# Moving the operands of a decoder layer's products by 16, 64 and 128 bytes in SBUF

## The chip, the cores and the metric

The kernel runs on one core of a Trainium2 chip. The metric is the device time of one execution in microseconds; a run's figure is the median over several executions. TensorE is PE in the profile (PEld its weight loads), VectorE is DVE, ScalarE is ACT, GpSimd is POOL, SyncE is SP.

## The reference

One decoder layer on 512 tokens of width 1024, all in float32: a shared RMS norm, one combined input projection, eight heads of block-sparse attention and four of differential attention, an output projection with a residual, and a SwiGLU feed-forward with 2816 hidden columns. The change touches where the feed-forward's operands lie, so its lines matter most:

```python
h = rms_norm(x, attn_norm[l])
proj = jnp.einsum('bsd,de->bse', h, w_in[l])
...
mixed = jnp.concatenate([moba_out, diff_out], axis=-1)
x = x + jnp.einsum('bse,ed->bsd', mixed, w_out[l])
h = rms_norm(x, ffn_norm[l])
g = jnp.einsum('bsd,df->bsf', h, w_gate[l])
u = jnp.einsum('bsd,df->bsf', h, w_up[l])
x = x + jnp.einsum('bsf,fd->bsd', jax.nn.silu(g) * u, w_down[l])
```

## The kernel before

Every float32 product is made of three matmuls on parts: an operand is split into a high part (a rounded copy, written by ACT) and a low part (the rest, written by DVE), and `product` issues high by high (line 1575), high by low (1576) and low by high (1577). Each of the three loads a 128 by 128 block of weights into the array (the stationary operand) and streams the other operand past it (the moving one). So each matmul reads two places of SBUF at about the same time: its moving operand, and the weights of the matmul behind it.

The weight parts lie in two rings of four slots, `w_hi` (WH) and `w_lo` (WL), 1024 float32 to a slot and partition. Product n uses slot n modulo 4 of both. ACT writes a slot of WH as soon as PE is done with its last user, DVE then the same slot of WL. The engines run written-out programs and wait on semaphores; no scheduler orders them.

Three stages follow each other on PE:

1. Projections and attention. Weights are slots 0 to 2 of the rings, the moving operand is `h_parts` (H1), 512 columns at a time. Short attention matmuls lie between. The output projection then takes `mixed_parts` (MIX) as weights, and ring slots, `w_out_parts` or H1 as the moving operand.
2. Gate and up, 78 products of 24 matmuls (1872 in all) by a seven-product scheme in `gate_product` and `first_product`. Weights are ring slots; the moving operand is 256 tokens of `h_first_parts` (A1: products Q1 and Q2) or one of five sums in `h_sum_parts` (SC: index 0 for Q6, 1 for Q5, 2 for Q7, 3 for Q3, 4 for Q4). Ten of the eleven units run all seven products; in each of them three, Q5, Q7 and Q3, use the sums 1, 2 and 3. The first unit's eight products run plainly, four of them on A1, two on sum 3 and two on sum 4. Beside PE, DVE and ACT split the weights of the products to come and add blocks of weights (`w_sum`).
3. Down, 42 steps in `down`. Here the hidden activations' parts, `hidden_parts` (AR), are the weights and the ring slots are the moving operand, 512 columns at a time.

Tensors are placed by hand, one behind the other, with byte offsets in a partition. `place` hands out the next offset or takes one that is given; `r0` is the offset of H1:

```python
WH, at_wh = place("w_hi", [P, 4, D], F32R)
WL, at_wl = place("w_lo", [P, 4, D], F32R)
...
SHIFT = 320
SC, _ = place("h2_sum_parts", [P, 5, 2, KTH, HALF], F32R, r0 + SHIFT)
A1, _ = place("h2_first_parts", [P, 2, KT, HALF], F32R, r0 + 106 * KB + SHIFT)
AR, _ = place("hidden_parts", [P, SLOTS, 2, SEQ], F32R, r0 + 106 * KB + 512)
```

A block of weights is 512 bytes of a partition, a moving operand 1024 bytes (256 columns) or 2048 bytes (512 columns), and the blocks and operands within a slot or a sum follow each other at these distances. Worked out from the first offset, 16512, each operand begins at these remainders of 512 bytes: WH and WL 128 in all four slots, H1, MIX, `w_out_parts` and AR 128, SC 448 in all five sums, A1 448.

Of the kernel before, what the change touches and what calls it, by code (L numbers as in the profile page):

```python
# [36 lines left out]
F32 = mybir.dt.float32  # L37
F32R = mybir.dt.float32r
U32 = mybir.dt.uint32

P = 128
SEQ = 512
D = 1024
# [5 lines left out]
KT = D // P  # L49
PAIRS = 8  # L50
MOBA_PAIRS = 4
FT = FFN // P
# [33 lines left out]
HALF = SEQ // 2  # L86
KTH = KT // 2
SLOTS = 4

assert FT % 2 == 0  # L90
assert SEQ // BLOCK == 2, "MoBA is causal attention for two blocks only"

# [54 lines left out]
def build(nc, x, wt, vec, gain2, lams, ident_in, mask_in, cos_in, sin_in, out):  # L147
    with ExitStack() as ctx:
        cursor = [16512]

        def place(name, shape, dt, at=None):

            n = 4
            for s in shape[1:]:
                n *= s
            if at is None:
                at = cursor[0]
                cursor[0] += n
            return nc.alloc_sbuf_tensor_at(name, shape, dt, offset=at), at

        def sem(name):
            return ctx.enter_context(nc.semaphore(name))


        X, _ = place("residual", [P, TT, D], F32)
        RAW, _ = place("w_raw", [P, 4, D], F32)
        WH, at_wh = place("w_hi", [P, 4, D], F32R)
        WL, at_wl = place("w_lo", [P, 4, D], F32R)
        ident, _ = place("ident", [P, P], F32)
        mask, _ = place("mask", [P, P], F32)  # L170
        cosT, at_cos = place("cos", [P, SEQ], F32)
        sinT, _ = place("sin", [P, SEQ], F32)
        small, _ = place("small", [P, 256], F32)

        QG, at_tmp = place("q_gained", [P, SEQ], F32)
        QR, _ = place("q_rotated", [P, SEQ], F32)
        QS, _ = place("q_roped", [P, SEQ], F32)
        KG, _ = place("k_gained", [P, SEQ], F32)
        KR, _ = place("k_rotated", [P, SEQ], F32)
        KS, _ = place("k_roped", [P, SEQ], F32)  # L180
        VT, _ = place("v_by_dim", [P, SEQ], F32)
        C1, _ = place("q1_kept", [P, SEQ], F32, at_tmp)
        V3, _ = place("q167_kept", [P, SEQ], F32, at_tmp + 2048)
        V2A, _ = place("q16_kept_0", [P, SEQ], F32, at_tmp + 2 * 2048)
        G0, _ = place("gate_first", [P, SEQ], F32, at_tmp + 3 * 2048)
        T1, _ = place("w_sum_1", [P, D], F32, at_tmp + 4 * 2048)
        U1, _ = place("up_second", [P, SEQ], F32, at_tmp + 6 * 2048)
        WO, _ = place("w_out_parts", [P, 2, D], F32R, at_tmp)


        KB = 1024
        SHIFT = 320
        H1, r0 = place("h_parts", [P, KT, 2, SEQ], F32R)
        MIX, r1 = place("mixed_parts", [P, KT, 2, SEQ], F32R)
        SC, _ = place("h2_sum_parts", [P, 5, 2, KTH, HALF], F32R, r0 + SHIFT)
        LATE = [place(f"down_raw_{n}", [P, D], F32, r0 + (4 * n if n < 5 else 34) * KB)[0] for n in range(6)]
        SN, _ = place("hidden_sums", [P, UNITS, HALF], F32, r0 + 22 * KB)
        RAW1, _ = place("w_raw_odd", [P, 4, D], F32, r0 + 40 * KB + SHIFT)
        G1, _ = place("gate_second", [P, SEQ], F32, r0 + 56 * KB + SHIFT)
        U0, _ = place("up_first", [P, SEQ], F32, r0 + 58 * KB + SHIFT)  # L200
        V2B, _ = place("q16_kept_1", [P, SEQ], F32, r0 + 60 * KB + SHIFT)
        HID, _ = place("hidden", [P, FT, SEQ], F32, r0 + 62 * KB + SHIFT)
        A1, _ = place("h2_first_parts", [P, 2, KT, HALF], F32R, r0 + 106 * KB + SHIFT)
        AR, _ = place("hidden_parts", [P, SLOTS, 2, SEQ], F32R, r0 + 106 * KB + 512)
        T2, _ = place("w_sum_2", [P, D], F32, at_cos)
        V2 = (V2A, V2B)
        r2 = r1 + 32 * KB
        VF, _ = place("v_turned", [P, TT, P], F32, r2)
        QF, _ = place("q_ready", [P, SEQ], F32, r2 + 8 * KB)
        KF, _ = place("k_ready", [P, SEQ], F32, r2 + 10 * KB)  # L210
        SQQ, _ = place("q_squared", [P, SEQ], F32, r2 + 16 * KB)
        SQK, _ = place("k_squared", [P, SEQ], F32, r2 + 18 * KB)
        MSR, _ = place("mean_square_rows", [P, 2, HALF], F32, r2 + 2 * KB)
        KBC, _ = place("k_rstd_spread", [P, TT, 2, HEAD], F32, r2 + 20 * KB)
        ON, _ = place("o_normed", [P, TT, P], F32, r2 + 22 * KB)
        LAM0, _ = place("lambda_in", [P, 4 * HEAD], F32, r2 + 22 * KB)

        HN2, _ = place("h2_normed", [P, TT, D], F32, r2)
        JUNK2, _ = place("squares2", [P, D], F32, r2 + 16 * KB)
        G2, _ = place("ffn_gain", [P, D], F32, r2 + 20 * KB)  # L220

        r3 = r2 + 24 * KB
        H2R, _ = place("h2_by_dim", [P, KT, SEQ], F32, r3)
        SR, _ = place("h2_sums", [P, 4, KTH, HALF], F32, r2 + 2 * KB + SHIFT)
        PT, _ = place("probsT", [P, 2, TT, SEQ], F32, r3)
        JUNK, _ = place("squares", [P, 2, D], F32, r3 + 16 * KB)

        PR0, _ = place("probs_0", [P, 2, SEQ], F32, at_wh + 3 * 4 * D)
        PR1, _ = place("probs_1", [P, 2, SEQ], F32, at_wl + 3 * 4 * D)
        PR = (PR0, PR1)  # L230


# [53 lines left out]
        w_hi = sem("w_hi_ready")  # L286
        w_lo = sem("w_lo_ready")
# [1831 lines left out]
```

## Time and profile before

| what | value |
|---|---|
| median of 3 runs | 602.42 us (602.38 to 602.43) |
| span of the profiled execution | 600.4 us |
| PE busy (matmuls) | 592.0 us, 99% of the span |
| PEld busy (weight loads) | 507.4 us, 85% |
| DVE busy | 471.8 us, 79% |
| ACT busy | 315.3 us, 53% |
| POOL busy | 28.1 us, 5% |
| instructions | 10407, of them 3820 matmuls |

The profile is of one execution. Its time is given by its span alone, from the first instruction to the end of the last; the 2.0 us between 600.4 and the runs' median lie around the program and are in no row. A matmul's row gives its start and a modelled end, and neighbours overlap, so busy time says little about pace. The pace is read from the starts: the distance between two matmuls' starts, divided by the matmuls between them.

### The profile page before, as it was taken

The page shows a single profiled execution, that of the slowest core. Times are in us where ns is not written, and L with a number is a line of the kernel's source. Part 1 is how long each engine was busy: PE and PEld are TensorE (multiplying, and loading weights), DVE is VectorE, ACT ScalarE, POOL GpSimd, SP SyncE. Part 2 cuts the span into 40 slices and gives each one's busy share as a digit, 9 for nine tenths or more (in the row PEclk, how much of TensorE's full clock was granted, in tenths as well). Part 3 has the DMA queues.
Part 4 walks back from the last instruction along what each step waited for, and adds up shares of the span by engine and source line. Part 5 has one row for each costly group of instructions (what it writes and reads, how often), then busy time and mean ns, then how long its engine had stood idle before and what let it go on. Part 6 is the DMA issues. An engine that isn't in the chain of part 4 may idle for free.

```text
span 600.4 us, 10407 instructions
## 1 busy us (share of the span) xinstructions
PE 592.0 (99%) x3820; PEld 507.4 (85%) x3820; DVE 471.8 (79%) x769; ACT 315.3 (53%) x545; POOL 28.1 (5%) x28
## 2 busy tenths in 40 slices
PE   8999999999999999999999999999999999999997
PEld 7766776776777777889999999999999998888886
DVE  4877777776797977677977788778877877999774
ACT  6555647375464646346554445453544365556551
POOL 0000000000000000000000000000000022155200
PEclk9999999999999999999999999999999999999999
DMA  8414132240412243308132243223422479699911
GB/s 298 124 58 136 41 102 70 70 136 6 139 52 89 70 175 106 106 2 281 36 118 80 86 141 134 77 73 141 139 71 73 142 180 264 182 190 206 187 36 70
DMA packets 33240, 70.31 MB, mean 117 GB/s; under 512 B 3376, under 2 KB 3760, under 8 KB 33200
## 3 DMA queue, kind: packets, MB, share of 16 engines
q1 hardware_dynamic: 26896, 58.14, 28.6%
q0 software_dynamic: 6016, 11.54, 10.9%
q8 instruction: 27, 0.44, 0.3%
q14 instruction: 13, 0.11, 0.1%
q10 hardware_dynamic: 288, 0.08, 0.1%
HBM read 63.45 MB, written 2.10 MB: 109 GB/s over the span
## 4 chain that ended last, share of the span: by engine, by line
PE 88%; DVE 6%; ACT 2%; issue 2%; SPq 1%; DMA 1%; DVEq 0%; ACTq 0%
PE ps L1575 26%; PE ps L1576 25%; PE ps L1577 25%; PE ps L1662 2%; PE ps L1680 2%; PE ps L1697 2%; PE ps L1705 1%; DVE small L1100 1%; ACT probs L664 1%; SPq L469 1%; PE ps L1741 1%; DVE probs L1128 1%; DVE ps L1094 1%; PE ps L1932 1%; PE ps L1751 1%
## 5 line engine op out<-in xcount | busy, mean ns | idle before, releaser
L1575 PE MATMUL ps<-h_sum_parts,w_hi 128*128 128x256 f32 x432 | 120.6, 279 | 0.7 <-ACT q_kept L866 0.7
L1576 PE MATMUL ps<-h_sum_parts,w_hi 128*128 128x256 f32 x432 | 120.9, 280 | 0.0
L1577 PE MATMUL ps<-h_sum_parts,w_lo 128*128 128x256 f32 x432 | 120.5, 279 | 0.0
L1575 PEld LDWEIGHTS ps<-h_sum_parts,w_hi 128*128 128x128 f32 x432 | 81.2, 188 | 0.9 <-ACT q_kept L866 0.9
L1576 PEld LDWEIGHTS ps<-h_sum_parts,w_hi 128*128 128x128 f32 x432 | 81.1, 188 | 0.0
L1577 PEld LDWEIGHTS ps<-h_sum_parts,w_lo 128*128 128x128 f32 x432 | 80.8, 187 | 0.0
L1575 PE MATMUL ps<-h_parts,w_hi 128*128 128x512 f32 x190 | 77.9, 410 | 0.3 <-DVE h_parts L1171 0.3
L1577 PE MATMUL ps<-h_parts,w_lo 128*128 128x512 f32 x190 | 74.5, 392 | 0.0
L1576 PE MATMUL ps<-h_parts,w_hi 128*128 128x512 f32 x190 | 74.1, 390 | 0.0
L664 ACT ACTIVATE probs<-ps,small 128x128 f32<-128x128 f32 (+3 forms) x64 | 38.9, 614 | 45.9 <-DVE small L1105 45.8
L1576 PE MATMUL ps<-w_lo,hidden_parts 128*128 128x512 f32 x154 | 59.9, 389 | 0.0
L1575 PE MATMUL ps<-w_hi,hidden_parts 128*128 128x512 f32 x154 | 59.9, 389 | 0.0
L1577 PE MATMUL ps<-w_hi,hidden_parts 128*128 128x512 f32 x154 | 59.9, 389 | 0.0
L1576 PE MATMUL ps<-h_first_parts,w_hi 128*128 128x256 f32 x192 | 53.8, 280 | 0.0
L1575 PE MATMUL ps<-h_first_parts,w_hi 128*128 128x256 f32 x192 | 53.7, 280 | 0.0
L1577 PE MATMUL ps<-h_first_parts,w_lo 128*128 128x256 f32 x192 | 53.6, 279 | 0.0
L1024 DVE TENSOR_TENSOR w_lo<-w_raw,w_hi 128x1024 fp32r<-128x1024 f32 x29 | 35.3, 1222 | 16.4 <-ACT w_hi L616 16.4
L1575 PEld LDWEIGHTS ps<-h_parts,w_hi 128*128 128x128 f32 x190 | 35.7, 188 | 10.2 <-issue 4.0
L1577 PEld LDWEIGHTS ps<-h_parts,w_lo 128*128 128x128 f32 x190 | 35.7, 188 | 8.0
L1576 PEld LDWEIGHTS ps<-h_parts,w_hi 128*128 128x128 f32 x190 | 35.8, 189 | 6.3
L1024 DVE TENSOR_TENSOR w_lo<-w_raw_odd,w_hi 128x1024 fp32r<-128x1024 f32 x25 | 30.6, 1223 | 13.2 <-ACT w_hi L616 13.2
L561 POOL DMA_DIRECT2D w_raw_odd<-wt x12 | 14.6, 1214 | 522.3 <-DVE w_lo L1415 522.3
(189 smaller groups left out, 1232.9 us busy)
## 6 DMA issues: line engine op xcount, KB each, us to landing
w_raw<-wt SPq DMA_DIRECT2D x59, 512.0 KB, 4.5
w_raw_odd<-wt SPq DMA_DIRECT2D x24, 512.0 KB, 4.2
w_raw_odd<-wt POOLq DMA_DIRECT2D x12, 512.0 KB, 7.4
down_raw<-wt SPq DMA_DIRECT2D x6, 512.0 KB, 9.5
w_raw<-wt POOLq DMA_DIRECT2D x5, 512.0 KB, 10.2
residual<-x SPq DMA_DIRECT2D x4, 512.0 KB, 5.1
q_rotated<-q_gained SPq DMA_DIRECT2D x32, 64.0 KB, 2.0
k_rotated<-k_gained SPq DMA_DIRECT2D x32, 64.0 KB, 2.0
```

Source lines behind the costliest of these rows:

```text
L469: sp.dma_start(dst[32 * b:32 * b + 32], src[32 * (b ^ 1):32 * (b ^ 1) + 32]).then_inc(done, 16)
L561: pool.dma_start(down_raw("B11", c).rearrange("p (f n) -> p f n", n=SEQ), down_rows(role, c), accum_op=ALU.add).then_inc(tb_added[c], 16)
L664: nc.scalar.activation(PR[qt % 2][:, a, 0:W], ps[:, 2 + a, at:at + W], ACT.Exp, bias=NB[:, i:i + 1], scale=RQ[:, i:i + 1], accum_out=SUM[: ...
L1024: nc.vector.tensor_tensor(WL[:, n % SLOTS], product_source(n), WH[:, n % SLOTS].bitcast(F32), ALU.subtract).then_inc(c_lo, 1)
L1094: nc.vector.tensor_tensor(diagonal, diagonal, mask[:].unsqueeze(1).unsqueeze(1).broadcast_to([P, 2, blocks, P]), ALU.add).then_inc(masked, 1)
L1100: ins = nc.vector.tensor_reduce(MX[:, 2 * qt:2 * qt + 2], ps[:, 2:4, s0:s0 + (qt + 1) * P], AX.X, ALU.max)
L1575: nc.tensor.matmul(dst, lh, rh, start=start, stop=False, skip_group_check=True)
L1576: nc.tensor.matmul(dst, lh, rl, start=False, stop=False, skip_group_check=True)
L1577: return nc.tensor.matmul(dst, ll, rh, start=False, stop=stop, skip_group_check=True)
L1662: ins = nc.tensor.matmul(ps[:, 2 + a, at:at + W], QF[rows[a], qt * P:W], KF[rows[a], 0:W], start=True, stop=True, skip_group_check=True)
L1680: ins = nc.tensor.transpose(ps[:, bank, at + kt * P:at + (kt + 1) * P], PR[qt % 2][:, a, kt * P:(kt + 1) * P], ident[:])
L1697: ins = nc.tensor.matmul(ps[rows, 6, qs], VF[:, kt, rows], PT[:, a, kt, qs], start=kt == 0, stop=kt == TT - 1, skip_group_check=True)
```

## The change

No instruction is added, removed or moved: on every engine the program's rows are the same, in the same order, and only line numbers differ by up to eight. What changes is addresses. The slots of both rings lie 4160 bytes apart and no longer 4096. The five sums of SC lie 8208 bytes apart and no longer 8192. What lies above SC in the same region (`w_raw_odd`, `gate_second`, `up_first`, `q16_kept_1`, `hidden` and A1) is 128 bytes higher, in which the 80 bytes that SC grows by find room. A gap of 256 bytes behind each ring makes all that follows move by 1024 bytes together.

In remainders of 512 bytes: slots 0 to 3 of WH and of WL now begin at 128, 192, 256, 320; the sums 0 to 4 of SC at 448, 464, 480, 496, 0; A1 at 64. H1, MIX, `w_out_parts` and AR stay at 128. The distance of the moving operand from the weights, in the same remainders, was 320 in stage 2 and 0 in stages 1 and 3. It is now 320 less 64 for each slot and more by 16 for each sum (448 less 64 for each slot with A1) in stage 2, and a multiple of 64 from 0 to 192, by the slot, in those parts of stages 1 and 3 that use the rings. Sums 1, 2 and 3 are the only ones that no longer begin at a multiple of 64 bytes.

```diff
+STEP = 16
+APART = 4
...
-        WH, at_wh = place("w_hi", [P, 4, D], F32R)
-        WL, at_wl = place("w_lo", [P, 4, D], F32R)
+        WH_, at_wh = place("w_hi", [P, 4, D + STEP], F32R)
+        cursor[0] += 4 * 4 * STEP
+        WL_, at_wl = place("w_lo", [P, 4, D + STEP], F32R)
+        cursor[0] += 4 * 4 * STEP
+        WH, WL = WH_[:, :, 0:D], WL_[:, :, 0:D]
...
-        SC, _ = place("h2_sum_parts", [P, 5, 2, KTH, HALF], F32R, r0 + SHIFT)
+        SC_, _ = place("h2_sum_parts", [P, 5, 2 * KTH * HALF + APART], F32R, r0 + SHIFT)
+        SC = SC_[:, :, 0:2 * KTH * HALF].rearrange("p i (a k q) -> p i a k q", a=2, k=KTH)
...
-        RAW1, _ = place("w_raw_odd", [P, 4, D], F32, r0 + 40 * KB + SHIFT)
+        RAW1, _ = place("w_raw_odd", [P, 4, D], F32, r0 + 40 * KB + SHIFT + 128)
...
-        A1, _ = place("h2_first_parts", [P, 2, KT, HALF], F32R, r0 + 106 * KB + SHIFT)
+        A1, _ = place("h2_first_parts", [P, 2, KT, HALF], F32R, r0 + 106 * KB + SHIFT + 128)
...
-        PR0, _ = place("probs_0", [P, 2, SEQ], F32, at_wh + 3 * 4 * D)
-        PR1, _ = place("probs_1", [P, 2, SEQ], F32, at_wl + 3 * 4 * D)
+        PR0, _ = place("probs_0", [P, 2, SEQ], F32, at_wh + 3 * 4 * (D + STEP))
+        PR1, _ = place("probs_1", [P, 2, SEQ], F32, at_wl + 3 * 4 * (D + STEP))
```

## Rows read from the trace of the kernel before

**Rows 1.** The page, parts 1 and 2: busy time, and the granted clock in slices.

```profile
PE 592.0 (99%) x3820; PEld 507.4 (85%) x3820; DVE 471.8 (79%) x769; ACT 315.3 (53%) x545; POOL 28.1 (5%) x28
...
PEclk9999999999999999999999999999999999999999
```

**Rows 2.** Windows by stage: us; busy PE, PEld, DVE, ACT, POOL; granted clock; DMA.

```profile
0.00:20.00 20.00, 18.18 (x92) 15.96 (x93) 11.32 (x23) 12.56 (x21) 0.20 (x4) 1.00 0.69 250
20.00:269.00 249.00, 246.31 (x1378) 182.64 (x1378) 192.18 (x461) 133.11 (x308) 0.00 (x0) 1.00 0.28 87
269.00:486.00 217.00, 217.00 (x1842) 216.75 (x1841) 176.08 (x183) 108.96 (x133) 0.00 (x0) 1.00 0.32 112
486.00:492.50 6.50, 5.81 (x50) 5.74 (x50) 5.12 (x8) 4.16 (x7) 2.54 (x2) 1.00 1.02 256
492.50:601.00 108.50, 104.68 (x462) 86.34 (x460) 87.08 (x99) 56.49 (x78) 25.35 (x22) 1.00 0.74 164
```

**Rows 3.** Timeline of PE in stage 2, start and us; 189 starts apart.

```profile
300.02 0.28 PE L1575 MATMUL ps<-h_sum_parts,w_hi 128*128 128x256 f32 x1
...
322.28 0.28 PE L1575 MATMUL ps<-h_sum_parts,w_hi 128*128 128x256 f32 x1
```

**Rows 4.** Tile h_sum_parts from 310 to 470: duration in ns, min/median/max.

```profile
L1575 PE MATMUL ps<-h_sum_parts,w_hi x324: 279/279/279, 310.6 to 470.0; 128*128 128x256 f32 x162
L1576 PE MATMUL ps<-h_sum_parts,w_hi x323: 280/280/280, 310.7 to 469.7; 128*128 128x256 f32 x162
L1577 PE MATMUL ps<-h_sum_parts,w_lo x323: 279/279/279, 310.9 to 469.9; 128*128 128x256 f32 x162
```

**Rows 5.** Timeline of PE, end of stage 2; the last two are 42 starts apart.

```profile
485.64 0.28 PE L1576 MATMUL ps<-h_sum_parts,w_hi 128*128 128x256 f32 x1
485.76 0.28 PE L1577 MATMUL ps<-h_sum_parts,w_lo 128*128 128x256 f32 x1
486.72 0.39 PE L1575 MATMUL ps<-h_sum_parts,w_hi 128*128 128x256 f32 x1 [0.69 <-ACT q_kept L866]
486.94 0.28 PE L1576 MATMUL ps<-h_sum_parts,w_hi 128*128 128x256 f32 x1
487.06 0.28 PE L1577 MATMUL ps<-h_sum_parts,w_lo 128*128 128x256 f32 x1
487.17 0.28 PE L1575 MATMUL ps<-h_sum_parts,w_hi 128*128 128x256 f32 x1
...
491.93 0.28 PE L1575 MATMUL ps<-h_sum_parts,w_hi 128*128 128x256 f32 x1
```

**Rows 6.** Tile h_sum_parts from 487.5 to 492: duration in ns.

```profile
L1576 PE MATMUL ps<-h_sum_parts,w_hi x14: 276/276/276, 487.3 to 491.7; 128*128 128x256 f32 x14
L1577 PE MATMUL ps<-h_sum_parts,w_lo x14: 276/276/276, 487.4 to 491.8; 128*128 128x256 f32 x14
```

**Rows 7.** Timeline of PE, first matmuls of stage 3; the last row is the twelfth.

```profile
492.27 0.39 PE L1575 MATMUL ps<-w_hi,hidden_parts 128*128 128x512 f32 x1
492.50 0.40 PE L1576 MATMUL ps<-w_lo,hidden_parts 128*128 128x512 f32 x1
492.74 0.39 PE L1577 MATMUL ps<-w_hi,hidden_parts 128*128 128x512 f32 x1
492.97 0.40 PE L1575 MATMUL ps<-w_hi,hidden_parts 128*128 128x512 f32 x1
493.20 0.39 PE L1576 MATMUL ps<-w_lo,hidden_parts 128*128 128x512 f32 x1
...
494.79 0.39 PE L1577 MATMUL ps<-w_hi,hidden_parts 128*128 128x512 f32 x1
```

**Rows 8.** Timeline of PE near the end, 444 starts behind the last row above.

```profile
595.43 0.39 PE L1577 MATMUL ps<-w_hi,hidden_parts 128*128 128x512 f32 x1
```

More of the change, by code:

```diff
@@ L194, in build @@
         MIX, r1 = place("mixed_parts", [P, KT, 2, SEQ], F32R)
-        SC, _ = place("h2_sum_parts", [P, 5, 2, KTH, HALF], F32R, r0 + SHIFT)
+        SC_, _ = place("h2_sum_parts", [P, 5, 2 * KTH * HALF + APART], F32R, r0 + SHIFT)
+        SC = SC_[:, :, 0:2 * KTH * HALF].rearrange("p i (a k q) -> p i a k q", a=2, k=KTH)
         LATE = [place(f"down_raw_{n}", [P, D], F32, r0 + (4 * n if n < 5 else 34) * KB)[0] for n in range(6)]
         SN, _ = place("hidden_sums", [P, UNITS, HALF], F32, r0 + 22 * KB)
-        RAW1, _ = place("w_raw_odd", [P, 4, D], F32, r0 + 40 * KB + SHIFT)
[L199 to L202, printed above, removed]
-        A1, _ = place("h2_first_parts", [P, 2, KT, HALF], F32R, r0 + 106 * KB + SHIFT)
+        RAW1, _ = place("w_raw_odd", [P, 4, D], F32, r0 + 40 * KB + SHIFT + 128)
+        G1, _ = place("gate_second", [P, SEQ], F32, r0 + 56 * KB + SHIFT + 128)
+        U0, _ = place("up_first", [P, SEQ], F32, r0 + 58 * KB + SHIFT + 128)
+        V2B, _ = place("q16_kept_1", [P, SEQ], F32, r0 + 60 * KB + SHIFT + 128)
+        HID, _ = place("hidden", [P, FT, SEQ], F32, r0 + 62 * KB + SHIFT + 128)
+        A1, _ = place("h2_first_parts", [P, 2, KT, HALF], F32R, r0 + 106 * KB + SHIFT + 128)
         AR, _ = place("hidden_parts", [P, SLOTS, 2, SEQ], F32R, r0 + 106 * KB + 512)
```

## The prediction

> **What bounds the kernel now.** First the page: PE is busy for 592.0 of 600.4 us, and its granted clock stands at 9 tenths or more in every slice [rows 1]. So PE bounds the kernel, at its upper level of 2.4 GHz, and the question is whether it is at its best pace.
>
> Then the windows by stage [rows 2]. In stage 2 (269 to 486 us) PE has work for all of 217.0 us, its weight loads for 216.75, DVE for 176 and ACT for 109. DVE has 19% to spare, so no other engine sets the pace there. In stage 3 (492.5 on) PE is again without gaps until the end, and its loads are busy for 86 of 108.5 us. The clock is 1.00 in each window.
>
> Then the starts of matmuls. In stage 2, 189 starts take 322.28 - 300.02 = 22.26 us: 117.78 ns for a matmul of 256 columns [rows 3]. It is the same everywhere: from 310 to 470 us the three kinds of matmul have durations of 279, 280 and 279 ns from minimum to maximum, whatever slot, sum or block they read and whatever DVE and ACT do beside them [rows 4].
>
> But one piece of stage 2 runs faster. Before product Q4 of the last unit PE waits: its last start before is 485.76, the next 486.72, released by ACT's copy of Q7's result. From 487.17 to 491.93 then, 42 starts take 4.76 us: 113.33 ns each [rows 5], and the duration is 276 ns [rows 6]. These are the same instructions, on the same rings and sums at the same remainders of addresses, with the same clock. So **there are two paces for the same matmul**, 4.45 ns apart, and each keeps itself up: the slow one through more than 1800 matmuls, the fast one, after a restart, until the stage ends.
>
> Stage 3 shows what a disturbance costs where the moving operand has 512 columns. From 494.79 to 595.43, 444 starts take 100.64 us, 226.67 ns each, which is twice 113.33 [rows 7, 8]. Its first matmuls come at distances of 0.23, 0.24, 0.23 and 0.23 us, and the first eleven take 494.79 - 492.27 = 2.52 us, where eleven at the even pace take 2.493. So PE needs a few matmuls to settle after the switch from stage 2, and pays some 27 ns for it [rows 7].
>
> **The change, part by part.** Nothing is executed more or less, and no wait moves, so all of it is in the pace at which a pair of reads, weights and moving operand, gets through. The trace of before cannot show what another distance between the two does: all of stage 2 has one distance (320, in remainders of 512), all of stages 1 and 3 another (0). Each cost is therefore bounded from both paces.
>
> Stage 2 at the fast pace. Of 1872 matmuls the last 48 run fast already. The other 1824 give back at most 1824 x 4.45 ns = 8.1 us. The lower bound is 0, and on the side of a loss a second step of the same size, 4.45 ns a matmul. I take the whole 8.1 us as the first term: the slow pace lived on unbroken sameness, and a restart was enough to end it. With the change the distance moves at all 77 switches from one product to the next, since the slot moves on by 64 bytes each time and the sum by 16, 32 or 48 bytes at most switches. That is a disturbance per 24 matmuls, and of the two paces the one that two products of other slot and sum shared without a break [rows 5] is the one that I expect to be found and kept.
>
> What the switches cost. A settling of 27 ns [rows 7] at each of 77 switches is 2.1 us. Bounds: 0 (the switch between the last two products, within rows 5, leaves 113.33 untouched) and twice as much, 4.2 us. I take 2.1, since now the distance changes too.
>
> Stage 3. The ring slots are the moving operand, and the distance changes at each of 41 switches between 42 steps. The even pace of 226.67 may stay for all distances; a settling of 27 ns at each switch costs 1.1 us. Bounds: 0 and 2.2 us. I take 1.1.
>
> Stage 1. The projections' three blocks of a pair change slot too, but attention matmuls break them up already and PE settles anew after each break, so I take 0, with up to 24 x 27 ns = 0.6 us against it.
>
> The other moves cost nothing: `w_raw_odd`, `hidden`, `gate_second`, `up_first`, `q16_kept_1` and the two tiles of probabilities are read by DVE, ACT, PE's transposes and DMA as before. If DVE's or ACT's instructions grew by a few per cent, the 41 us that DVE has free in stage 2 [rows 2] would hide it. A faster PE asks DVE for 176 us of work in some 211 instead of 217, which leaves 35. The wait before the last unit's Q4, 0.96 us from start to start, follows from PE's own result and ACT's copy of it [rows 5], and stays.
>
> The sum: -8.1 + 2.1 + 1.1 = -4.9 us. Against the profiled execution, 600.4 - 4.9 = 595.5 us of span; with the 2.0 us by which the median of the runs lies above that span, 597.5 us.
>
> A page speaks against all this. What the rows show: one matmul, two paces, with no other engine's work to tell them apart [rows 4, 5]. The Trainium skill, "SBUF — State Buffer", section "Who interferes with whom", says that PE has two read ports, one for the moving operand and one for weights, independent of each other, and that PE never waits on anyone there. By it no address matters, the sum would be 0 and the time 602.4. The trace does not contradict it outright, since no row has the same stage at two distances; but two ports without any interplay leave the second pace unexplained.
>
> **The rivals.**
>
> *No change.* The paces depend on how PE entered the stage, not on where the operands lie; 117.78 ns stays. For it: both paces occur at the same addresses [rows 3, 5], and the small stop within the first product, for transposes, did not bring the fast one, since rows 3 come after it. Against it: at a fixed distance nothing could shake the pace off. It gives 602.4 us, within 0.2%, which is about what a measurement of this kernel can tell from no change.
>
> *Slower: the sums off the 64-byte grid.* The sums 1, 2 and 3 begin 16, 32 and 48 bytes behind a multiple of 64, which no operand of PE does before. If a moving row that straddles such a multiple costs one more step of 4.45 ns, the 32 products on these sums pay 768 x 4.45 = 3.4 us, and if no fast pace comes to pay for it, the time is 605.8. It decides from 1.6 ns a matmul on (1.2 us, the 0.2%). For it: the kernel's only even paces were measured with everything on that grid. Against: the rows know just two paces and no third.
>
> *All of it.* The fast pace comes and the switches cost nothing, as between the last two products: 602.4 - 8.1 = 594.3 us.
>
> *A part.* Only some products leave the slow pace, say those of one or two slots of four, a quarter to a half of 8.1 us, less the switches: about 600.
>
> **How the numbers follow.** The forecast (fast pace with settling) has a chance of 0.40, its own range 594.3 to 600.5, the latter if settling costs twice the terms above (8.1 - 6.4 = 1.7). All of it 0.10, a part 0.08, no change 0.17, slower 0.25. Faster by over 0.2% takes the first three, 0.58; same is 0.17; slower 0.25. The range runs from 593.8, a little under the full gain, to 605.8, the slower rival's own time; it leaves out some 0.15, most of it losses larger than one step, as in stage 3, where 462 matmuls at 4.45 ns more would add 2.1 us.
>
> **What would show each step.** The first term: in the profile after, starts of stage 2 at 113.3 ns and durations of 276 ns for most products. Settling: one to five uneven distances behind each switch of product or step, and an even pace between. The slower rival: Q5, Q7 and Q3 alone at more than 117.8 ns. No change: 279 and 280 ns as before. The prediction is wrong if the fast pace needs the old distance: then every product has a pace of its own by slot and sum, and the time is a mean over them that no row of before holds.

## The result and the profile after

The changed kernel takes 606.05 us (605.27 to 606.23, 4 runs) against 602.4 us (601.7 to 602.43, 4 runs) for the kernel before: 1.0062 times, 95% interval 1.005 to 1.0074. It is slower by 0.6%; 597.5 us were predicted. The profiled execution is the fastest of the four (605.27), so the traces show 3.1 us of the 3.65 between the medians.

The page, parts 1 and 2, as in [rows 1]:

```profile
PE 595.7 (99%) x3820; PEld 507.0 (84%) x3820; DVE 472.2 (78%) x769; ACT 315.5 (52%) x545; POOL 28.1 (5%) x28
...
PEclk9999999999999999999999999999999999999999
```

PE is busy for 3.7 us more, DVE and ACT for 0.4 and 0.2, and the clock stands as before. So PE's own matmuls grew. Where they did is read from windows that end at the first matmul of each stage (columns as in [rows 2]). First the changed kernel, then the kernel before:

```profile
10.55:269.79 259.24, 257.33 (x1416) 190.31 (x1417) 201.76 (x479) 140.56 (x321) 0.00 (x0) 1.00 0.28 91
269.79:493.33 223.54, 222.85 (x1890) 222.65 (x1888) 180.82 (x189) 113.19 (x139) 2.54 (x2) 1.00 0.34 116
493.33:603.50 110.17, 106.96 (x464) 86.55 (x462) 87.45 (x99) 56.54 (x78) 25.32 (x22) 1.00 0.73 161
```

```profile
10.67:269.29 258.62, 255.67 (x1416) 189.94 (x1417) 201.59 (x479) 140.47 (x321) 0.00 (x0) 1.00 0.29 91
269.29:492.27 222.98, 222.29 (x1889) 222.09 (x1888) 180.69 (x189) 113.08 (x139) 2.54 (x2) 1.00 0.34 116
492.27:600.40 108.13, 104.91 (x464) 86.53 (x462) 87.31 (x99) 56.52 (x78) 25.35 (x22) 1.00 0.75 165
```

Stage 1 is 0.62 us longer, stage 2 0.56, stage 3 2.04. Together, with a start 0.12 earlier, that is the 3.1 us between the spans of 600.4 and 603.5. PE's waits did not grow: in each stage the busy time rose by as much as the length, or by more.

The tile `h_sum_parts` from 310 to 470 us, which answers to [rows 4], and `hidden_parts` from 495 to 595; duration in ns, minimum/median/maximum:

```profile
L1583 PE MATMUL ps<-h_sum_parts,w_hi x322: 275/281/288, 311.1 to 470.0; 128*128 128x256 f32 x161
```

```profile
L1583 PE MATMUL ps<-w_hi,hidden_parts x145: 388/394/398, 494.7 to 594.6; 128*128 128x512 f32 x145
```

Where one duration stood before, a whole band stands now, 13 ns wide in stage 2. What lies in it is seen in the timeline of PE (start and us). The first six rows are three pairs, each 15 starts apart within one product on `h_first_parts`: product 20 on ring slot 0, product 27 on slot 3, product 34 on slot 2. The last six are the first matmuls of steps of stage 3, 12 starts apart, on slots 2, 3, 0, 1, 2 and 3:

```profile
328.86 0.28 PE L1583 MATMUL ps<-h_first_parts,w_hi 128*128 128x256 f32 x1
...
330.56 0.28 PE L1583 MATMUL ps<-h_first_parts,w_hi 128*128 128x256 f32 x1
...
348.64 0.28 PE L1583 MATMUL ps<-h_first_parts,w_hi 128*128 128x256 f32 x1
...
350.44 0.28 PE L1583 MATMUL ps<-h_first_parts,w_hi 128*128 128x256 f32 x1
...
368.51 0.28 PE L1583 MATMUL ps<-h_first_parts,w_hi 128*128 128x256 f32 x1
...
370.21 0.28 PE L1583 MATMUL ps<-h_first_parts,w_hi 128*128 128x256 f32 x1
...
493.33 0.39 PE L1583 MATMUL ps<-w_hi,hidden_parts 128*128 128x512 f32 x1
...
496.11 0.39 PE L1583 MATMUL ps<-w_hi,hidden_parts 128*128 128x512 f32 x1
...
498.91 0.39 PE L1583 MATMUL ps<-w_hi,hidden_parts 128*128 128x512 f32 x1
...
501.65 0.40 PE L1583 MATMUL ps<-w_hi,hidden_parts 128*128 128x512 f32 x1
...
504.41 0.40 PE L1583 MATMUL ps<-w_hi,hidden_parts 128*128 128x512 f32 x1
...
507.21 0.39 PE L1583 MATMUL ps<-w_hi,hidden_parts 128*128 128x512 f32 x1
```

15 starts take 1.70 us (113.3 ns each) in product 20, 1.80 us (120.0) in product 27, and 1.70 again in product 34. The three products read the same half, so one moving operand has different paces on different ring slots. In stage 3 the steps take 2.80 us on slot 3 (233.3 ns), 2.74 on slot 0 (228.3), 2.76 on slot 1 (230.0) and 2.80 on slot 2, where the even pace of before was 226.67 [rows 8].

**The theories.** The distance theory (D): the pace of a matmul follows from the distance between its moving operand and the weights, taken in remainders of some power of two, and lasts as long as that distance does. Its rivals: only the switches cost (each change of slot or sum brings a settling, and the pace between is as before); a moving operand off the 64-byte grid costs a step; and, for the two paces of before, a stop of PE ends the slow one. Distance below is the moving operand's first byte less the weights' first byte, as a remainder of 512 unless another is named.

### The profile page after: what moved, and what is told of

It is laid out like the page before. It is cut to its first block, busy times and chain, and to the rows that moved or that the text cites. A ratio compares the mean times of both kernels' runs of the same rounds, so it can differ in the third digit from the quotient of the medians.

```text
span 603.5 us, 10407 instructions
## 1 busy us (share of the span) xinstructions
PE 595.7 (99%) x3820; PEld 507.0 (84%) x3820; DVE 472.2 (78%) x769; ACT 315.5 (52%) x545; POOL 28.1 (5%) x28
## 4 chain that ended last, share of the span: by engine, by line
PE 88%; DVE 6%; ACT 2%; issue 1%; DMA 1%; SPq 1%; DVEq 0%; ACTq 0%
PE ps L1583 26%; PE ps L1585 26%; PE ps L1584 26%; PE ps L1670 3%; PE ps L1688 2%; PE ps L1705 2%; PE ps L1713 1%; DVE small L1108 1%; ACT probs L672 1%; DMA residual<-x 1%; DVE probs L1136 1%; DVE ps L1102 1%; PE ps L1627 1%; PE ps L1940 1%; PE ps L1654 1%
```

## The experiments

### e1: the rings alone

The slots of the rings 64 bytes further apart, the sums and `h2`'s first half where they were. Against the changed kernel:

```diff
-APART = 4
+APART = 0
...
-        A1, _ = place("h2_first_parts", ..., r0 + 106 * KB + SHIFT + 128)
+        A1, _ = place("h2_first_parts", ..., r0 + 106 * KB + SHIFT)
```

> The rings' slots stand 64 bytes further apart, the sums and the first half stay where they were. Theory D (a matmul's pace is set by the distance from its weights to its moving operand, in remainders of 512 bytes): stages 1 and 3 lose what they lose with the whole change (0.6 and 2.1 us); in stage 2 the products run at 117.8, 120.0, 117.7 or 113.4, and 118.8 ns for slots 0 to 3, which adds 1.5 us or takes 0.5: 604.6 to 606.6 in all. Theory S (my prediction's: every switch of distance costs a settling of some 27 ns, and an even distance costs nothing): 77 and 41 switches, 605 to 606. Theory G (only operands off the 64-byte grid are slow): nothing is off the grid, so stage 2 keeps 117.8 and the time is 602.4 if stage 3 keeps its pace too.

604.85 us (604.62 to 605.31) against 601.94: 1.0047 (1.003 to 1.0063). The timeline of PE at the first matmuls of five products in a row, 24 starts apart, on slots 0, 1, 2, 3 and 0:

```profile
328.49 0.28 PE L1583 MATMUL ps<-h_first_parts,w_hi 128*128 128x256 f32 x1
...
331.32 0.28 PE L1583 MATMUL ps<-h_sum_parts,w_hi 128*128 128x256 f32 x1
...
334.20 0.28 PE L1583 MATMUL ps<-h_first_parts,w_hi 128*128 128x256 f32 x1
...
336.93 0.28 PE L1583 MATMUL ps<-h_sum_parts,w_hi 128*128 128x256 f32 x1
...
339.77 0.28 PE L1583 MATMUL ps<-h_sum_parts,w_hi 128*128 128x256 f32 x1
```

The products take 2.83, 2.88, 2.73 and 2.84 us. Their distances are 320, 256, 192 and 128, and every product of a slot has its slot's pace, whatever sum it reads: 117.8, 120.0, 113.3 and 118.7 ns in the even part (the intervals repeat in a short pattern, on slot 1 for example 121, 120, 124, 118, 117 ns, and the pace is the mean over whole patterns). The four nearly cancel: stage 2 is 222.82 us long, 222.98 before. Stage 3, where the distance goes 0, 64, 128, 192, is 110.17 us, just as after the whole change. So the rings alone hold the loss of stage 3, and all operands here lie on the 64-byte grid. The time by itself fits the theory of switches as well (605 to 606); what decides against it is that the paces differ in the even parts, between the switches.

### e2: the sums alone

The complement: the sums 16 bytes further apart and `h2`'s first half 128 further on. Against the changed kernel:

```diff
-STEP = 16
+STEP = 0
```

> The sums stand 16 bytes further apart and the first half 128 bytes further on, the rings are as before. D: stages 1 and 3 are as before, since their distances are; in stage 2 sum 0 runs at 117.8, sum 1 at 119.7, sum 2 at 119.9, sum 3 at 113.3, sum 4 at 119.0 and the first half at 117.8 or 113.4 ns, a mean of 117.9 or 116.7: 602.7 or 600.4. S: some 50 switches in stage 2, 1.4 us, 603.8. G: sums 1 to 3 alone are slower, each by the same step, others keep 117.8.

601.58 us (600.61 to 602.1): 0.9994 (0.9984 to 1.0003). PE's timeline at the first matmuls of Q3 (sum 3), Q6 (sum 0), Q5 (sum 1), Q7 (sum 2) and the product behind them:

```profile
335.08 0.28 PE L1583 MATMUL ps<-h_sum_parts,w_hi 128*128 128x256 f32 x1
...
337.84 0.28 PE L1583 MATMUL ps<-h_sum_parts,w_hi 128*128 128x256 f32 x1
...
340.67 0.28 PE L1583 MATMUL ps<-h_sum_parts,w_hi 128*128 128x256 f32 x1
...
343.55 0.28 PE L1583 MATMUL ps<-h_sum_parts,w_hi 128*128 128x256 f32 x1
...
346.43 0.28 PE L1583 MATMUL ps<-h_first_parts,w_hi 128*128 128x256 f32 x1
```

2.76, 2.83, 2.88 and 2.88 us at distances 368, 320, 336 and 352. Now the pace goes with the sum and not with the slot. Of the three sums off the grid, two are slower than before and one, sum 3, is the fastest (113.3 ns in its even part, with some 35 ns a product for settling). The off-grid rival asked for all three to be slower, and so falls. The time lies between the two that D had named, since `h2`'s first half, at 448, runs at 113.3 ns in 12 of its products and at 117.8 in the others. Stage 3 is 108.10 us, as before.

### e3: one distance, 368, for all of stage 2

If the distance decides, then all products at the distance of sum 3 are fast, with no slot moved. The kernel before with the sums and `h2`'s first half at a remainder of 496 (their neighbours are moved out of the way by `SHIFT`; `SC` and `A1` are views that begin 4 floats into their tensors):

```diff
-        SHIFT = 320
+        SHIFT = 512
...
-        SC, _ = place("h2_sum_parts", [P, 5, 2, KTH, HALF], F32R, r0 + SHIFT)
+        SC_, _ = place("h2_sum_parts", [P, 5 * 2 * KTH * HALF + 4], F32R, r0 + 352)
+        SC = SC_[:, 4:4 + 5 * 2 * KTH * HALF].rearrange("p (i a k q) -> p i a k q", i=5, a=2, k=KTH)
```

> The rings are as before; all five sums and the first half begin at a distance of 368 instead of 320 from every slot, off the 64-byte grid. D: stage 2 runs at 113.3 ns throughout, as sum 3 on slot 0 does in the changed kernel, and gives back 8.1 us: 594.3. S: no switch changes the distance, so stage 2 stays at its 117.8: 602.4. G: every operand is off the grid, 1872 x 2 ns or more slower than before: 606 or above.

594.18 us (593.85 to 594.4): 0.9867 (0.9851 to 0.9884). Tile `h_sum_parts`, 310 to 470 us, and the window of stage 2 (columns as in [rows 2]):

```profile
L1577 PE MATMUL ps<-h_sum_parts,w_hi x336: 275/275/275, 309.7 to 469.9; 128*128 128x256 f32 x168
```

```profile
269.16:484.51 215.35, 214.61 (x1889) 214.21 (x1888) 180.39 (x189) 113.22 (x139) 2.54 (x2) 1.00 0.35 120
```

The fast pace holds from product to product: one takes 2720 ns, 24 times 113.33, and stage 2 is 215.35 us long, 7.6 less than before. Switches between products cost nothing here, and "unbroken sameness" does no harm.

### e7 and e10: 16 bytes less, and 256 bytes less

The same kernel with one number changed each: e7 at distance 352, e10 at 112.

```diff
-        SC = SC_[:, 4:4 + 5 * 2 * KTH * HALF]...
+        SC = SC_[:, 0:0 + 5 * 2 * KTH * HALF]...
```

```diff
-        SC_, _ = place("h2_sum_parts", [P, 5 * 2 * KTH * HALF + 4], F32R, r0 + 352)
+        SC_, _ = place("h2_sum_parts", [P, 5 * 2 * KTH * HALF + 4], F32R, r0 + 96)
```

(`A1` likewise in both.)

> As the even distance of 368, but 352: 16 bytes less, for all sums and the first half. D: 119.9 ns for 1872 matmuls, as sum 2 on slot 0, 4.0 us above before and 12 above the distance of 368: about 606. S, and a theory that the mere move of the sums brought the 8 us back: as with 368, 594, or as before, 602.

> As the even distance of 368, but 112, which is 256 less. Where distances of 0 and 256, and of 64 and 320, met in the profiles so far they had the same pace, so D in remainders of 256 gives stage 2 the 113.3 ns of 368 and a time of 594.2. D in remainders of 512 alone gives 112 a pace of its own, anything from 113.3 to 120.4: 594 to 607.

e7: 605.8 us (605.53 to 606.12), 1.0067 (1.005 to 1.0084). e10: 594.18 us (593.75 to 594.37), 0.9872 (0.9856 to 0.9889). Tile `h_sum_parts`, e7 and then e10, with the window of stage 2 in e7 between:

```profile
L1577 PE MATMUL ps<-h_sum_parts,w_hi x320: 279/282/286, 311.0 to 469.0; 128*128 128x256 f32 x160
```

```profile
268.93:496.25 227.32, 226.63 (x1890) 226.43 (x1888) 181.03 (x189) 113.39 (x139) 2.54 (x2) 1.00 0.34 114
```

```profile
L1577 PE MATMUL ps<-h_sum_parts,w_hi x336: 275/275/275, 309.7 to 469.9; 128*128 128x256 f32 x168
```

16 bytes are worth 605.8 - 594.18 = 11.6 us: e7's products take 2880 ns, 24 times 120.0. So it is not the mere move of the tensors that brought e3 its gain. And 256 bytes change nothing, so the remainder that counts is that of 256 (or of a divisor: but 128 apart the paces differ, 112 and 240 below).

### e5: stage 3 at one other distance

The kernel before with `hidden_parts` at distance 192 throughout; the ring slots stay:

```diff
-        AR, _ = place("hidden_parts", [P, SLOTS, 2, SEQ], F32R, r0 + 106 * KB + 512)
+        AR, _ = place("hidden_parts", [P, SLOTS, 2, SEQ], F32R, r0 + 106 * KB + SHIFT)
```

> The kernel before, with the hidden parts 192 bytes lower, so that every step of stage 3 has a distance of 192 instead of 0; nothing changes from step to step. D: 233.3 ns for each of 462 matmuls, as on slot 3 in the changed kernel, 3.1 us more than before, about 605. S: no switch of distance, so 226.7 ns and no difference.

604.92 us (604.65 to 605.45): 1.0052 (1.0036 to 1.0069). Tile `hidden_parts`, 495 to 590 us:

```profile
L1576 PE MATMUL ps<-w_lo,hidden_parts x136: 394/394/394, 494.8 to 589.3; 128*128 128x512 f32 x136
```

The pace is 233.3 ns at every step, as on slot 3 of the changed kernel, where the other operand had moved, and the stage takes 111.15 us instead of 108.13. No slot and no step differs from its neighbours here, so a loss without any switch is shown: 462 x (233.33 - 226.67) = 3.1 us.

### e4: the whole change, with stage 3's distance held at 0

The four slots of `hidden_parts` become four tensors, each at its ring slot's remainder:

```diff
-        AR, _ = place("hidden_parts", [P, SLOTS, 2, SEQ], F32R, r0 + 106 * KB + 512)
+        AR = [place(f"hidden_parts_{t}", [P, 2, SEQ], F32R, r0 + 106 * KB + 512 + 4160 * ((t + 2) % SLOTS))[0] for t in range(SLOTS)]
```

> The whole change, and each of the four slots of the hidden parts moved by as much as the ring slot that it meets in stage 3, so that the distance in stage 3 is 0 at every step again, though both operands stand elsewhere from step to step. D and S alike: stage 3 is back at 226.7 ns, 2.1 us less than with the change, 604.0. G, or any theory by an operand's own address: stage 3 as with the change, 606.

605.12 us (605.09 to 605.66): 1.0054 (1.0037 to 1.007). Stage 3 takes 109.58 us, so only 0.6 of the 2.04 us came back, where 2.1 were expected: a miss. The first matmul of a step and the first of the next, from PE's timeline:

```profile
496.53 0.39 PE L1583 MATMUL ps<-w_hi,hidden_parts 128*128 128x512 f32 x1
...
499.29 0.39 PE L1583 MATMUL ps<-w_hi,hidden_parts 128*128 128x512 f32 x1
```

Twelve starts take 2.76 us (230.0 ns), and the unevenness behind a switch lasts about ten of them before 226.7 returns. The mean of the stage is 229.92, and (229.92 - 226.72) x 462 = 1.5 us, or 36 ns a switch. The time alone does not tell D from a theory by an operand's own address, which expected 606. The ends of the steps do: all four slots come back to 226.7, where the changed kernel stays at 232 to 233 on two of them. So a settling at switches is real. It comes even with the same distance on both sides, when both operands move by 64 bytes; in e3, where neither remainder moves, it is nil.

### e6 and e8: other distances in stage 3

e3 with the four slots of `hidden_parts` at four distances: 448, 368, 320, 256 in e6, and 96, 48, 32, 16 in e8. The question was whether any distance beats 226.67.

```diff
+        AR_AT, AR_IN = (576, 4736, 8896, 13056), (0, 4, 0, 0)
+        AR = [place(f"hidden_parts_{t}", [P, 2 * SEQ + AR_IN[t]], F32R, r0 + 106 * KB + AR_AT[t])[0][:, AR_IN[t]:]...
```

In e8 the two lists are `(928, 5056, 9184, 13280)` and `(0, 4, 0, 4)`.

> The even distance of 368 in stage 2, and in stage 3 the four slots of the hidden parts at distances of 448, 368, 320 and 256 from the ring slots, which no run has shown there. The profile is what is asked for: D expects a pace of its own for each slot, S 226.7 ns on all four behind a few uneven matmuls at each switch. A pace under 226.7 would show that stages 1 and 3 have something to gain as well. The time is that of the even distance, 594, and 1 to 3 us more.

> As the four distances, with 96, 48, 32 and 16 for the four slots of the hidden parts in stage 3. D: a pace for each slot, between 226.7 and 237 ns as so far. If one is under 226.7, stages 1 and 3 have room; if none is, 226.7 is the floor for 512 columns that the distances of the kernel before had already.

596.88 and 597.11 us, one run each, 2.7 and 2.9 above e3. PE's timeline in e6, first matmuls of steps at distances 448, 368, 320, 256 and 448 again, 12 starts apart:

```profile
484.97 0.40 PE L1579 MATMUL ps<-w_hi,hidden_parts 128*128 128x512 f32 x1
...
487.76 0.39 PE L1579 MATMUL ps<-w_hi,hidden_parts 128*128 128x512 f32 x1
...
490.56 0.39 PE L1579 MATMUL ps<-w_hi,hidden_parts 128*128 128x512 f32 x1
...
493.32 0.39 PE L1579 MATMUL ps<-w_hi,hidden_parts 128*128 128x512 f32 x1
...
496.04 0.40 PE L1579 MATMUL ps<-w_hi,hidden_parts 128*128 128x512 f32 x1
```

The step at 368 takes 2.80 us (233.3 ns): the best distance for 256 columns is among the worst for 512. The step at 256 takes 2.72 (226.7). e8's even paces are 233.3 at 96, 231.9 at 48, 233.3 at 32, and at 16 226.67 in some steps and 228.3 in others. None is under 226.67, so of the nine distances tried in stage 3 none beats the one that it had.

### e9: three stops

Whether a restart ends the slow pace, at the old distance of 320: the kernel before, with PE held at three products of stage 2 until weights that are due three products later are split:

```diff
-                pe.wait_ge(c_lo, n + 1)
+                pe.wait_ge(c_lo, n + (4 if n in (12, 33, 54) else 1))
```

> The kernel before, with addresses as they were, where PE waits in front of three products of stage 2 (at a sixth, a bit under a half, and two thirds of it) for weights that are three products ahead, so that it stands still for one to three us and starts anew each time. My prediction held that such a restart ends the slow pace of 117.8 ns: then stage 2 runs at 113.3 from the first stop on, some 6.5 us back, less three stops. The rival: what is reached behind a stop depends on where in its cycle PE starts, and 117.8 comes back behind some stops or all of them; with all of them the time is before plus the stops.

611.83 us (611.14 to 612.47): 1.0168 (1.015 to 1.0186). PE's waits show the stops (us in total, times, longest), and PE's timeline three pairs of starts, each 15 apart: behind the second stop, the third, and the stop before the last Q4 that the kernel before has too [rows 5]:

```profile
PE ps L1575 <- DVE w_lo L1024: 7.5, 3, 2.5
```

```profile
383.00 0.28 PE L1575 MATMUL ps<-h_sum_parts,w_hi 128*128 128x256 f32 x1
...
384.76 0.28 PE L1575 MATMUL ps<-h_sum_parts,w_hi 128*128 128x256 f32 x1
...
445.09 0.28 PE L1575 MATMUL ps<-h_sum_parts,w_hi 128*128 128x256 f32 x1
...
446.86 0.28 PE L1575 MATMUL ps<-h_sum_parts,w_hi 128*128 128x256 f32 x1
...
496.93 0.28 PE L1575 MATMUL ps<-h_sum_parts,w_hi 128*128 128x256 f32 x1
...
498.70 0.28 PE L1575 MATMUL ps<-h_sum_parts,w_hi 128*128 128x256 f32 x1
```

1.76, 1.77 and 1.77 us, where the fast pace makes 1.70. The slow pace comes back behind every stop, in this run even behind the one after which before had run fast. A restart does not end it. Of the 10.3 us that the run takes more than before, 7.5 are the waits and some 1.5 the low clock behind the first stop (last section).

e5 has all addresses that before has in stage 2, and its trace shows the same from the other side: the last Q7, then the same stop, then Q4. The first two and the last two starts are 15 apart:

```profile
483.51 0.28 PE L1575 MATMUL ps<-h_sum_parts,w_hi 128*128 128x256 f32 x1
...
485.21 0.28 PE L1575 MATMUL ps<-h_sum_parts,w_hi 128*128 128x256 f32 x1
...
486.74 0.39 PE L1575 MATMUL ps<-h_sum_parts,w_hi 128*128 128x256 f32 x1 [0.69 <-ACT q_kept L866]
...
487.20 0.28 PE L1575 MATMUL ps<-h_sum_parts,w_hi 128*128 128x256 f32 x1
...
488.97 0.28 PE L1575 MATMUL ps<-h_sum_parts,w_hi 128*128 128x256 f32 x1
```

1.70 us (113.3 ns) ahead of the stop, reached without a stop or a change of distance, and 1.77 (118.0) behind it. So at 320 PE can fall into either pace, and a stop ends the fast one as well. At 368 no trace shows such a choice: in e3, ten intervals of 115 to 121 ns follow behind this stop, and then 113.3 again.

### The paces by distance

Worked out from the starts of PE in the traces above, as the mean time between starts over whole patterns in the even part of a product or step, in ns. Distances are remainders of 256, since two distances 256 apart agreed within 0.2 ns wherever both occurred (192 and 448 of stage 2 in both of their paces):

| distance | 256 columns (stage 2) | 512 columns (stage 3) |
|---|---|---|
| 0 | 120.0 | 226.67 |
| 16, 32, 48 | 118.7, 116.7, 118.3 | 226.67 or 228.3, 233.3, 231.9 |
| 64 | 113.3 or 117.8 | 228.9 |
| 80, 96 | 120.0, 120.0 | 96: 233.3 |
| 112 | 113.3 | 233.3 |
| 128 | 118.7 | 232.4 |
| 144, 160, 176 | 118.7, 118.7, 119.2 | not tried |
| 192 | 113.3 or 117.8 | 233.3 |
| 208, 224, 240 | 119.1, 118.4, 117.1 | not tried |

Which of its two paces a product at 64 or 192 takes goes with the product before it. Behind one at 0, 32, 48, 96, 160 or 240 all 41 took the fast pace, and behind one at 112, 128 or 176 44 of 45 took the slow one.

## Why the prediction was wrong, point by point

**The first term, -8.1 us, failed.** Stage 2 got 0.56 us longer. The step that fails is "the slow pace lived on unbroken sameness, and a restart was enough to end it". e3 keeps a fast pace through a stage of perfect sameness, e9 restarts three times and gets the slow one back, and in e5 the very stop of [rows 5] ends the fast pace. What decides is the distance: e1 and e2 move one operand each, and the pace follows the slot in the one and the sum in the other. The change spreads stage 2 over all 16 multiples of 16 bytes within 256. Of 74 products without a stop in them, 11 run at 113.3 and 45 at 118.3 or more; their mean is 117.92, where 117.78 stood before, 0.3 us over 1872 matmuls. Another 0.2 us (48 x 4.45 ns) is the fast end of [rows 5], where the last two products now have slower distances.

The forecast was drawn from the one place with two paces [rows 3, 5], and that place was an exception: with 256 columns, 64 and 192 are the only distances that showed two paces, 113.3 and 117.8. The rest have one each. That the trace of before had the slow pace ahead of the stop and the fast one behind was chance: e5, with the same addresses, has them the other way round. The prediction's last sentence held the cause, "every product has a pace of its own by slot and sum", but no chance was put on it; those of the forecast and the rivals already add up to 1. Its other half is refuted: the fast pace does not need the old distance, since 112 has it always.

**Settling, +2.1 in stage 2,** was of no account there: the even parts make 117.92 and the whole products 117.93. Behind switches into a fast distance up to 38 ns are lost, and behind others a little is gained.

**Stage 3, +1.1, was mis-sized and had the wrong cause.** "The even pace of 226.67 may stay for all distances" is refuted by e5. The term measured 2.04 us, of which the even paces of the slots (226.67, 228.9, 232.4 and 233.3, mean 230.3) make (230.3 - 226.7) x 462 = 1.7, and settling the rest. The bounds were 0 and 2.2, and they held it. e4 shows that the settling is there all the same: with the distance held, it alone makes 1.5 us.

**Stage 1, 0,** measured +0.62, at the bound of 0.6 that was named. The stage is 259.24 to 259.70 us long in the three kernels with moved rings (the changed one, e1, e4) and 258.00 to 258.95 in the nine others, so it goes with the rings. The reason given for 0, that attention breaks the projections up already, does not hold. Between the breaks (starts that follow each other within 260 ns) the mean of the projections' starts rose from 228.5 to 233.0 ns on slot 1, at a distance of 192 in remainders of 256, and from 229.5 to 232.4 on slot 2, at 128, and hardly on slot 0, from 229.0 to 229.4. Those are, within 0.5 ns, the paces of stage 3 at these distances, and over the 480 starts they make 1.3 us; shorter waits took half of it back.

**The rivals.** "No change" is wrong, though near in stage 2, and for another reason: the paces by distance cancel there. Its condition, that the pace depends on how PE came in, holds at 64 and 192. "The sums off the 64-byte grid" gave 605.8 us, close to the measured time, by a mechanism that is refuted: e2 moves the sums off the grid and loses nothing, and e3 has every moving operand of stage 2 off it and is the fastest. The tiles and the other engines cost nothing, as said. One bound was added up wrongly: with settling at twice its terms the forecast is 602.4 - 8.1 + 6.4 = 600.7, not 600.5.

The Trainium skill, "SBUF — State Buffer", section "Who interferes with whom", has PE's two read ports independent and PE never waiting there. By it no address would matter, and the time would be 602.4. The runs here disagree: with nothing else changed, 16 bytes make 11.6 us of stage 2 (e3, e7) and 192 bytes 3.0 us of stage 3 (before, e5). The measurement decides.

**Open.** Why a distance has its pace, since no run looks into how the two reads meet; by what the product before, or a stop, chooses between the two paces at 64 and 192; what turned the slow pace into the fast one without a stop in e5; and why 256 columns are best at 112 where 512 are best at 0 and 16.

## What to carry to other kernels

When PE is busy without gaps and its starts come more slowly than the best seen for the same shape, vary the distance between moving operand and weights in SBUF, one remainder of 256 bytes for a whole stage, and measure. Here e3 and e10 are the fastest versions: 594.18 us, 1.3% under the kernel before, and 606.05 - 594.18 = 11.9 us under the changed one, by two offsets. Choose it for each shape by itself and keep it the same in all slots: a spread of distances brought only the mean of good and bad here. A distance that has one pace is the safer choice, since at 64 and 192 the same addresses gave the fast pace in one product and the slow one in the next.

## What the runs showed of the hardware

The pace of a matmul depends on the distance of its two reads, from 113.3 to 120.0 ns at 256 columns and from 226.67 to 233.3 at 512. In e3 the matmuls' durations are equal to the nanosecond for 160 us, while DVE and ACT go through their work beside them.

In e9 the clock fell behind one of the three stops. PE stopped from 315.8 to 318.6 us; the windows behind it (columns as in [rows 2]):

```profile
318.00:320.00 2.00, 1.41 (x12) 1.44 (x13) 1.58 (x2) 0.00 (x0) 0.00 (x0) 0.99 0.00 0
320.00:323.00 3.00, 3.00 (x17) 3.00 (x16) 0.00 (x0) 0.00 (x0) 0.00 (x0) 0.50 0.00 0
```

The granted clock is 0.50, the level of 1.2 GHz, only after PE was at work again, and matmuls start some 213 ns apart there. It was back by 323.4. The two later stops of the same length left the clock at its upper level in this execution. The mean granted clock of the four runs is 0.997, 0.997, 0.994 and 0.994, so in two of them about twice as much time passed at the lower level.
